# Gathered expert rows by quarters and VectorE block transposes, and modulation loads in other items of a two-layer diffusion step

## The reference

```
def layer_step(x, mod, rope, ctx_ckv, ctx_krope, p):
    sh1, sc1, g1, sh2, sc2, g2 = jnp.split(mod, 6, axis=-1)
    h = rmsnorm(x, p['norm1_g']) * (1 + sc1) + sh1
    mix, ckv, kpe = token_mixers(h, rope, ctx_ckv, ctx_krope, p)
    x = x + g1 * mix
    h = rmsnorm(x, p['norm2_g']) * (1 + sc2) + sh2
    x = x + g2 * expert_choice_ffn(h, p)
...
def expert_choice_ffn(h, p):
    cap = (EC_FACTOR * n) // N_EXPERTS          # 128 sample rows, 32 prompt rows per expert
    aff = jax.nn.softmax(h @ w_router)
    gates, idx = lax.top_k(aff.transpose(0, 2, 1), cap)
    xs = h[idx]
    hid = silu(xs @ w_gate) * (xs @ w_up)       # 16 experts, 1024 -> 512
    ye = (hid @ w_down) * gates
    out = zeros.at[idx].add(ye)
```

## Time and profile before

| | us |
|---|---|
| median of 3 runs (2449.34 to 2454.82) | 2451.83 |
| the profiled execution | 2456.23 |
| its span | 2454.5 |
| TensorE busy in the span | 2314.3 |
| VectorE busy | 744.8 |
| ScalarE busy | 513.2 |
| GpSimd busy | 279.4 |

### The profile page before, as it was taken

The page is one execution under the profiler, slowest core; times in us unless marked ns, Lnnn a source line. Parts: engine busy times, 40 slices in busy tenths (PEclk is TensorE's granted clock), DMA queues, the critical chain, the costliest instruction groups (busy, mean ns, idle before and its releaser), DMA issues.

```text
span 2454.5 us, 30238 instructions
## 1 busy us (share of the span) xinstructions
PE 2314.3 (94%) x12252; PEld 1517.4 (62%) x12252; DVE 744.8 (30%) x1409; ACT 513.2 (21%) x1050; POOL 279.4 (11%) x438
## 2 busy tenths in 40 slices
PE   6999997999799899999999999899999959999996
PEld 4545554555445787888765455456554448887885
DVE  2401244544236211111124012455523551111113
ACT  3310121222234211011033101222223320101003
POOL 2000011101000112111120000211100011112111
PEclk9999998999899999999999999999999979999998
DMA  9100279767425788888971002696642268888888
GB/s 333 35 4 18 66 161 216 163 136 138 180 95 190 272 271 282 276 271 270 346 247 35 7 15 68 141 203 122 134 126 95 86 229 274 272 275 280 275 278 298
DMA packets 216025, 440.70 MB, mean 180 GB/s; under 512 B 32033, under 2 KB 75225, under 8 KB 215937
## 3 DMA queue, kind: packets, MB, share of 16 engines
q1 hardware_dynamic: 169200, 360.28, 46.5%
q0 software_dynamic: 22928, 54.56, 9.4%
q10 hardware_dynamic: 23808, 24.66, 4.9%
HBM read 339.34 MB, written 47.65 MB: 158 GB/s over the span
## 4 chain that ended last, share of the span: by engine, by line
PE 84%; DMA 6%; DVE 4%; SPq 3%; ACT 1%; issue 1%; ACTq 1%; DVEq 0%; POOLq 0%
PE PS L1408 11%; PE PS L1415 11%; PE PS L1237 11%; PE PS L1440 9%; PE PS L1019 8%; PE PS L1169 6%; PE PS L973 6%; PE PS L1112 5%; PE PS L960 4%; DMA r<-r 4%; PE PS L1124 2%; PE PS L1434 2%; PE PS L1073 1%; PE PS L1393 1%; SPq L554 1%; DMA r<-in_x_sample_dram 1%
## 5 line engine op out<-in xcount | busy, mean ns | idle before, releaser
L1408 PEld LDWEIGHTS PS<-r,ring 128*128 128x128 f32 x2048 | 281.5, 190 | 16.0 <-issue 16.0
L1237 PE MATMUL PS<-ring,mix 128*128 128x512 f32 x640 | 289.0, 599 | 0.0
L1408 PE MATMUL PS<-r,ring 128*128 128x160 f32 x2048 | 283.6, 299 | 1.2 <-ACT r L1731 1.2
L1415 PE MATMUL PS<-r,ring 128*128 128x160 f32 x2048 | 283.4, 299 | 0.0
L1415 PEld LDWEIGHTS PS<-r,ring 128*128 128x128 f32 x2048 | 279.9, 190 | 0.0
L1440 PE MATMUL PS<-ring,r 128*128 128x512 f32 x496 | 221.2, 599 | 0.0
L1019 PE MATMUL PS<-r,ring 128*128 128x512 f32 (+1 forms) x576 | 208.4, 521 | 1.6 <-ACT r L1532 1.6
L1237 PEld LDWEIGHTS PS<-ring,mix 128*128 128x128 f32 x640 | 117.5, 191 | 128.8 <-issue 128.6
L1169 PE MATMUL PS<-r 128*128 128x256 f32 x768 | 176.6, 388 | 21.1 <-DMA r<-r 21.1
L1112 PE MATMUL PS<-lat,r 128*128 128x512 f32 (+1 forms) x416 | 188.7, 588 | 7.7 <-ACT ring L1594 5.1
L1169 PEld LDWEIGHTS PS<-r 128*128 128x128 f32 x768 | 149.0, 195 | 56.9 <-DMA r<-r 24.4
(11 more groups left out here) (304 smaller groups left out, 2184.9 us busy)
## 6 DMA issues: line engine op xcount, KB each, us to landing
ring<-in_w_gate_dram SPq DMA_DIRECT2D x32, 2048.0 KB, 10.1
ring<-in_w_up_dram SPq DMA_DIRECT2D x32, 2048.0 KB, 11.7
ring<-in_w_down_dram SPq DMA_DIRECT2D x31, 2048.0 KB, 9.4
ring<-in_w_ada_dram SPq DMA_DIRECT2D x15, 2048.0 KB, 9.8
r<-ring SPq DMA_DIRECT2D x144, 96.0 KB, 6.1
r<-r SPq DMA_DIRECT2D x128, 96.0 KB, 5.3
r<-r ACTq DMA_DIRECT2D x128, 96.0 KB, 5.5
r<-ring ACTq DMA_DIRECT2D x112, 96.0 KB, 5.8
```

Source lines behind the costliest of these rows:

```text
L1237: ins = pe.matmul(psum(2 * (s % 2) + n, 512), mix[:, k, tile * P:(tile + 1) * P], W_OUT[n][:, k, :], start=(k == 4), stop=(k == 3))
L1408: ins = pe.matmul(PS[:, b // 2, (b % 2) * 256:(b % 2) * 256 + SLOTS], W_G[:, k, b * P:(b + 1) * P], XST[par][:, k, :], start=(k == 0), sto ...
L1415: ins = pe.matmul(PS[:, 2 + b // 2, (b % 2) * 256:(b % 2) * 256 + SLOTS], W_U[:, k, b * P:(b + 1) * P], XST[par][:, k, :], start=(k == 0), ...
```

## The change

- `xn_dram` holds a row's channels in another order: VectorE writes `XN` so that quarter q of a row has channels 32q to 32q + 31 of each of the eight blocks of 128. One expert's rows are fetched by four indirect transfers of 128 pieces of 1 KB (`xn_quarters`): transfer g brings, for slots 32g to 32g + 31, quarter j to partitions 32j to 32j + 31. One VectorE instruction transposes the 32x32 blocks of `XS` into the 1024 columns behind it (`XSQ`), and this is already the turned form; ScalarE and VectorE modulate from there instead of from PSUM. TensorE's eight transposes are gone.
- The piece numbers `idx_4` are made by sixteen products of K = 32 that spread the merged list over the partitions, and one VectorE instruction; `route_ready` comes behind them. The prompt's turns 0 and 1 stand behind these products, and turn 2 behind `route_ready`.
- VectorE's loop body now has the turn and the modulation of rows e + 1 ahead of `hidden` of expert e.
- The chunks of modulation fall in items 0, 1, 3, 5, 7, 9, 11 and 13 (`CHUNK_ITEMS`) instead of 0 to 7; in layer 1 in 0, 1, 3 and 5. The `W_OUT` loads follow in the items of the last two chunks.
- The late chunks 0, 1 and 4 are issued in tiles 2, 3 and 4 of the projection loop, each behind the load of the tile after next.

```diff
+CHUNK_ITEMS = [0, 1, 3, 5, 7, 9, 11, 13]
+def chunk_at(l, n):
+    return CHUNK_ITEMS.index(n) if n in CHUNK_ITEMS[:len(ADA_ITEMS[l])] else -1
...
+        XSQ = r2[:, D:2 * D].rearrange("p (g c t) -> p c g t", g=4, c=KD)
...
+        xn_quarters = xn_dram.rearrange("t (q c) -> (t q) c", q=4)
...
                 for n in range(NI):
-                    load_ada_weights(n + 2)
+                    i = chunk_at(l, n)
+                    if i >= 0:
+                        load_ada_weights(i + 2)
                     exchange(n, (0, 1) if n < NI - 1 else range(4))
-                    load_ada_bias(n + 2)
-                    if n == len(ADA_ITEMS[l]):
+                    if i >= 0:
+                        load_ada_bias(i + 2)
+                    if i == len(ADA_ITEMS[l]) - 2:
...
                 load_xd(1)
-                if l == 0:
-                    sp.wait_ge(uvh_summed, at(l, NU, NU))
-                    load_tail_chunk(0)
-                    load_tail_chunk(1)
-                    load_tail_chunk(4)
                 for t in range(NT):
...
                     if t + 2 < NT:
                         load_xd(t + 2)
+                    if l == 0 and 2 <= t <= 4:
+                        sp.wait_ge(uvh_summed, at(l, NU, NU))
+                        load_tail_chunk((0, 1, 4)[t - 2])
...
                 def first_gather(e):
-                    pool.indirect_dma_start(XS, None, xn_dram, bass.IndirectOffsetOnAxis(idx_g[:, e:e + 1], 0))\
-                        .then_inc(xs_landed, 16)
+                    for g in range(4):
+                        pool.indirect_dma_start(XS[:, 256 * g:256 * (g + 1)], None, xn_quarters,
+                                                bass.IndirectOffsetOnAxis(idx_4[:, e, g:g + 1], 0)).then_inc(xs_landed, 16)
...
+                pe.wait_ge(lists_ready, at(l, 2, 2))
+                for g in range(4):
+                    own = slice(32 * g, 32 * g + 32)
+                    for j in range(4):
+                        ins = pe.matmul(PS[32 * j:32 * j + 32, g, 64:64 + E], ident[own, own], merge[own, 1, :],
+                                        start=True, stop=True)
+                ins.then_inc(top_turned, 1)
...
-                turn_rows(0)
                 turn_prompt_rows(3)
                 def expert(e, par, last=False):
...
-                    if not last:
-                        turn_rows(e + 1)
...
-                    dve.tensor_scalar(XN[s % 2], XO[s % 2], rstd[:, s:s + 1], None, ALU.mult).then_inc(xn2_ready, 1)
+                    dve.tensor_scalar(XN[s % 2].rearrange("p (q c r) -> p c q r", q=4, c=KD),
+                                      XO[s % 2].rearrange("p (c q r) -> p c q r", q=4, c=KD), rstd[:, s:s + 1], None,
+                                      ALU.mult).then_inc(xn2_ready, 1)
...
+                def turn_rows(n):
+                    dve.wait_ge(xs_landed, l * (64 * (E + 2)) + n * 64 + 64)
+                    dve.wait_ge(xst_ready, l * (E + 1) + n)
+                    dve.transpose(r2[:, D:2 * D], XS).then_inc(xs_turned, 1)
...
                 def expert(e, par):
+                    turn_rows(e + 1)
+                    modulate_rows(e + 1, 1 - par)
                     hidden(e, 0)
                     hidden(e, 1)
-                    modulate_rows(e + 1, 1 - par)
                     weigh_prompt(e)
```

More of the change, by code:

```diff
@@ L174, in backbone @@
         idx_s = sb("idx_s", [P, E], U32)
-        idx_g = sb("idx_g", [P, E + 2], U32)
+        idx_g = sb("idx_g", [P, E], U32)
+        idx_4 = sb("idx_4", [P, E + 2, 4], U32)
         idx_q = sb("idx_q", [P, 4], U32)
@@ L178, in backbone @@
         jcol = sb("jcol", [P, 1])
-        gcol = sb("gcol", [P, 1], U32)
+        gcol = sb("gcol", [P, 4], U32)
         scol = sb("scol", [P, 2], U32)
@@ L755, in _ @@
                 for n in range(NI - 1):
-                    store_gate(n)
+                    store_gate(chunk_at(l, n))
                     spread_inverses(n)
@@ L1199, in _ @@
                         scores(n, 0, c)
-                    turn_modulation(n - 1)
+                    turn_modulation(chunk_at(l, n - 1))
                     if n:
@@ L1208, in _ @@
                         times_values(n - 2, range(12))
-                    modulation(n)
+                    modulation(chunk_at(l, n))
                 n = NI - 1
@@ L1379, in _ @@
                 pe.transpose(PS[:, 0, 2 * E:4 * E], top_f[0:2 * E, CAP_P:SLOTS], ident[0:2 * E, 0:2 * E]).then_inc(top_turned, 1)
-                pe.wait_ge(lists_ready, at(l, 1, 1))
+                pe.wait_ge(lists_ready, at(l, 2, 1))
                 pe.matmul(PS[:, 1, 0:2 * E], flip[:, :], lists[:, :, E:2 * E], start=True, stop=True)\
                     .then_inc(top_turned, 1)
+                pe.wait_ge(lists_ready, at(l, 2, 2))
+                for g in range(4):
+                    own = slice(32 * g, 32 * g + 32)
[3 more added lines that the diff above has]
+                ins.then_inc(top_turned, 1)
                 turn_prompt_rows(0)
                 turn_prompt_rows(1)
+                pe.wait_ge(route_ready, at(l, 1, 1))
                 turn_prompt_rows(2)
                 pe.wait_ge(xsp_ready, at(l, 3, 2))
-                pe.wait_ge(route_ready, at(l, 1, 1))
-                def turn_rows(n):
-                    pe.wait_ge(xs_landed, l * (16 * (E + 2)) + n * 16 + 16)
-                    for k in range(KD):
-                        ins = pe.transpose(PS[:, 6 + k // 4, (k % 4) * P:(k % 4 + 1) * P], XS[:, k * P:(k + 1) * P],
-                                           ident[:, :])
-                    ins.then_inc(xs_turned, 1)
-                turn_rows(0)
                 turn_prompt_rows(3)
@@ L2020, in _ @@
                 for n in range(NI):
-                    copy_modulation(n - 1)
+                    copy_modulation(chunk_at(l, n - 1))
                     row_max(n, 0)
@@ L2027, in _ @@
                     invert_sums(n)
-                    bias_modulation(n)
+                    bias_modulation(chunk_at(l, n))
                 divide_out(NI - 4)
@@ L2161, in _ @@
                     .then_inc(top_ready, 1)
[L2162 removed]
+                dve.wait_ge(top_turned, at(l, 3, 1))
                 dve.tensor_copy(lists[:, :, :], PS[:, 0, 0:4 * E].rearrange("p (v e) -> p v e", v=2)).then_inc(lists_ready, 1)
[L2164 to L2165 removed]
+                dve.wait_ge(lists_ready, at(l, 2, 1))
+                dve.wait_ge(top_turned, at(l, 3, 2))
                 dve.tensor_tensor(gate_s[:, :], lists[:, 0, 0:E], PS[:, 1, 0:E], ALU.max)
@@ L2169, in _ @@
                 step(dve.tensor_tensor(merge[:, 1, :], merge[:, 1, :], merge[:, 0, :], ALU.mult))
-                step(dve.tensor_tensor(merge[:, 1, :], merge[:, 1, :], PS[:, 1, E:2 * E], ALU.add))
+                dve.tensor_tensor(merge[:, 1, :], merge[:, 1, :], PS[:, 1, E:2 * E], ALU.add).then_inc(lists_ready, 1)
+                dve.wait_ge(lists_ready, at(l, 2, 2))
                 dve.tensor_copy(idx_g[:, 0:E], merge[:, 1, :])
-                dve.tensor_scalar(idx_s[:, :], merge[:, 1, :], float(NP), None, ALU.add).then_inc(route_ready, 1)
+                dve.tensor_scalar(idx_s[:, :], merge[:, 1, :], float(NP), None, ALU.add)
+                dve.wait_ge(top_turned, at(l, 3, 3))
+                dve.tensor_scalar(idx_4[:, 0:E, :], PS[:, 0:4, 64:64 + E].rearrange("p g e -> p e g"), 4.0, jcol[:, :],
+                                  ALU.mult, ALU.add).then_inc(route_ready, 1)
                 dve.wait_ge(route_ready, at(l, 1, 1))
@@ L2220, in expert @@
                                              op0=ALU.mult, op1=ALU.mult).then_inc(ys_ready, 1)
+                turn_rows(0)
                 modulate_rows(0, 0)
```

25 lines of the change are left out of this document (11 added, 14 removed).

## The result

The changed kernel takes **2426.49 us**, median of four runs (2424.29 to 2431.10), against 2453.28 for the kernel before: ratio 0.9915, 95% interval 0.989 to 0.9939. That is 26.8 us less; 52.3 were forecast, and 2426.49 lies 0.5 us above the range. The profiled execution took 2425.75 us (span 2424.0, mean granted clock 0.969 against 0.975).

The account below looks back on a forecast made before the run. TensorE's work was taken to bound the kernel, with waits only outside the expert loop. Terms -28.5 + 13.6 - 23.4 + 1.5 - 15.5 = -52.3 us, from 2451.83 to 2399.5 us; range 2384 to 2426.

Parts of the forecast that it names:

- Attention of layer 0: Layer 0's attention: with chunk loads in every second item, TensorE's three idle stretches for exchanged blocks go; -23.4 us (-26 to -16).
- Rival (a): Layer 0's attention: exchanges stay late because the backlog forms in items 0 to 2; gives back 20, 2420 us; chance 0.12.
- The note at the end: Layer 0's attention: forecast is wrong if the idle stretches come back behind items 3, 5 and 7; no size given.
- a stall of 7 left: Layer 0's attention: cautious bound of that term, a gain of only 16 us with a stall of 7 us remaining.
- Expert loop: Both layers' experts: eight TensorE turns leave each of 31 rounds at 0.92 us; -28.5 us (-27.0 to -32.2).
- `hidden`'s cover of 0.3 us: Expert loop: second half of `hidden` still ends 0.3 us before the prompt's down product needs it, costing nothing.
- Start of the experts: Before expert 0 in each layer: list spreading, four gather issues, landing and turn lengthen the path; +13.6 us (+6 to +23).
- The clock's term of 1.5 a layer: Start of the experts: longer TensorE idleness lowers its clock and slows the following products; 1.5 us added per layer.
- Projection of layer 0: Layer 0's output projection: late loads moved behind tile loads no longer hold up a 31.14 us tile; -15.5 us.
- Attention of layer 1: Layer 1's attention: chunks 2 and 3 leave a stretch where TensorE waits anyway; +1.5 us (0 to +3).
- (b): Expert loop: transfer engines bind it, 384 more packets making rounds 28.4 us; 38 us longer, 2466 us; chance 0.07.
- (c): Expert loop: gathers land beyond their 22 us cover, `hidden` is late and TensorE waits; 155 us more, 2554 us; chance 0.02.

Follow-up runs that it names:

- the second profile: Profile of the changed kernel run once more, unaltered, on another chip against the kernel before: 2429.54 us against 2460.92, ratio 0.9878.

## Why the prediction was wrong

**Attention of layer 0, the step that failed** (forecast -23.4, measured +4.0 in the profiles, and nothing within some 12 us in the experiment with the chunks back). The miss of 27.4 us is more than the 21.8 by which the profiled executions fell short of the forecast sum; what the other terms missed comes to -5.6 together. The cause was named rightly: a chunk load ahead of the exchange. The step from it was wrong: "A chunk in every second item leaves the queue an item to drain, so I let the stretches go". The drained item comes after the load; the exchange that is late is the one issued 0.5 us behind it, and at items 5 and 9 it is late although the exchanges ahead of the load had their item to drain. A timeline of the kernel before could have warned of it: the exchanges that were waited for, those of items 2, 4 and 10, have a load 1.2, 0.5 and 6.6 us ahead of them. (The third is not "the same", as the prediction has it: `W_OUT`'s load is issued behind the exchange of its own item 9, and the next item's is the late one.) The schedule leaves an exchange some 21 us (item 7 of the changed kernel: issued 437.71, products at 458.73 without a wait), and behind a load it takes up to 28.5. Six exchanges stand directly behind a load before the change and six after it; the move changed their places and left the order, and with it the lateness. Rival (a) had this outcome, 2420 us with 0.12, but the wrong reason against it: that two of four loads ahead of an exchange are gone does not matter when the last one decides. The note at the end, that the idle stretches might come back behind items 3, 5 and 7, is what the second profile shows. The cautious bound of that term, "a stall of 7 left", should have reached a gain of nothing.

**Expert loop** (-28.5): 31 x 0.87 = -27.0, the low bound. The chain's price was right, and the larger start-to-start one was not. `hidden`'s cover of 0.3 us was there (0.37). VectorE waited for a gather once in each layer, in the first round (7.8 and 7.5 us), and `hidden` was not late for it; in the other rounds it never did.

**Start of the experts** (+13.6): the way to expert 0 grew by 0.6 and 1.7 us, its first gate product by 2.2 and 1.9; together +6.4, the low end. The sum added 3.84 us of later issues to the landing of the whole 512 KB gather; in fact the last quarter landed within 3.5 us of its issue, and VectorE began to turn the four 7.26 us after the first. The clock's term of 1.5 a layer was too small, since the first gate product ran at 0.79 in layer 0 and 0.83 in layer 1. The page DMA: Bandwidth & Descriptors of the Trainium skill, section "Anatomy of one DMA — SWDGE (gpsimd) path", fits 2.0 us plus the bytes at 436 GB/s to each DMA; taken four times, one after another, that is an estimate of 9.2 us for these gathers, and 3.2 us for the one before the change. The traces agree with neither: 7.26 us up to VectorE's start, and 6.60.

**What was costed at nothing:** the last experts of layer 0 wait 0.97 and 0.49 us for weights, and the way into layer 1 took 2.1 us longer. A faster loop gives its loads less time, and this is where two late chunks and the weights of layer 1 share the queue; the waits are in the kernels with the faster loop and in no other. The forecast had said that the slack falls by 0.9 us and had not looked at the one place where 4 MB more are loaded.

**Projection of layer 0** (-15.5): -15.5, right, and -17.3 (between -12 and -24) by itself in the kernel before. **Attention of layer 1** (+1.5): -0.4.

**Rivals.** (b), the transfer engines as the bound of the loop, did not happen: the software queue moved 438 packets in a round before and 480 after, where the rival had 384 more, and its time share rose from 17.8% of 27.19 us to 19.0% of 26.32, so by 0.2 us. The packets of 1 KB that the rival priced never came. All queues of one round, before and after:

```profile
DMA packets 3044, 7.47 MB, mean 275 GB/s; under 512 B 99, under 2 KB 231, under 8 KB 3044
```

```profile
DMA packets 3080, 7.46 MB, mean 283 GB/s; under 512 B 143, under 2 KB 271, under 8 KB 3080
```

Only the packets under 512 B are more, by 44; those from 512 B to 2 KB are 132 and 128. (c) did not happen.

## What to carry to other kernels

A small transfer that someone waits for goes ahead of a large load, and the load goes where its own use is far enough away; spreading loads while keeping the wrong order moved the waits here and removed none of their sum. When a stall is put down to what stands ahead of a transfer, ask whether the change alters that transfer's own neighbour, and let the term's bound reach to "nothing gained" until it does. Give an engine's idle time a filler (here the products of two chunks in the first items) before moving it away.

## What the runs showed of the hardware

- 96 KB of the exchange land 3.1 to 3.2 us after issue alone (item 11), and 12.3 to 17.0 behind a load of 2 MB (items 3, 5, 7 and 9, medians of SyncE's half). ScalarE's half, on another queue, is about as late as SyncE's, so the load holds up both queues. Part of the delay is not the load's bytes: for 8 us behind the load of item 9 only 40 GB/s moved, at a busy share of 0.64. How much comes from the order in one queue and how much from what the queues share was not separated; a load on a third queue was not run.
- A high busy share of the transfer engines is no sign that somebody waits for them, nor that much is moved: 0.94 at 202 GB/s with TensorE never waiting, 0.82 at 165 GB/s with TensorE idle for 15 of 135 us, 0.64 at 40 GB/s behind a load.
- Gathering rows of 4 KB as four quarters of 1 KB added 42 packets to a round of 438 of the software queue, all of them under 512 B. The number of packets from 512 B to 2 KB did not rise, so the pieces of 1 KB were not moved one to a packet.
- Attention of layer 0 took 253.2, 254.4, 259.8 and 264.5 us in four profiles with the loads in the same dense places. Where short exchanges race with large loads, one profile gives the kind of wait, and not its length to better than some 10 us.
